# A hybrid attention and delta-rule layer: the triangular inverse held in blocks of 32, with products on four row groups, and all queues in a new order

## The reference

```python
A = jnp.einsum('bhnid,bhnjd->bhnij', kb, k) * decay_strict   # 64x64, strictly lower
sys = A + jnp.eye(C)
u = triangular_solve(sys, v * beta)                          # unit diagonal
w = triangular_solve(sys, kb * exp(G))
def step(state, xs):
    v_new = u_c - w_c @ state
    o = q_c @ state + qk_c @ v_new
    state = state * gl + k_c.T @ v_new
```

## Time and profile before

| what | value |
|---|---|
| median of 3 runs | 191.32 us (190.97 to 197.76) |
| profiled execution, its own time | 190.73 us |
| its span, first to last instruction | 188.9 us |
| granted clock, mean | 0.996 |

### The profile page before, as it was taken

The page is one execution under the profiler, slowest core; times in us unless marked ns, Lnnn a source line. Parts: engine busy times, 40 slices in busy tenths (PEclk is TensorE's granted clock), DMA queues, the critical chain, the costliest instruction groups (busy, mean ns, idle before and its releaser), DMA issues.

```text
span 188.9 us, 4380 instructions
## 1 busy us (share of the span) xinstructions
PE 178.0 (94%) x1718; PEld 161.5 (85%) x1718; DVE 141.5 (75%) x345; ACT 101.5 (54%) x195; POOL 77.5 (41%) x42
## 2 busy tenths in 40 slices
PE   7999989889999998999999999999999999999980
PEld 6769879789999998998998999999998987888850
DVE  0359699893459988998999787889689777858074
ACT  2645444439368878956562270455384448636230
POOL 2036627335687922985055068224913200810000
PEclk9999999999999999999999999999999999999998
DMA  5999999999519980300901807006942983020023
GB/s 160 403 386 394 393 409 407 407 397 404 218 16 367 395 328 8 114 0 2 323 14 17 319 8 212 13 0 220 362 201 78 344 356 119 14 97 0 3 111 111
DMA packets 12246, 38.41 MB, mean 203 GB/s; under 512 B 1473, under 2 KB 1857, under 8 KB 11714
## 3 DMA queue, kind: packets, MB, share of 16 engines
q1 hardware_dynamic: 12082, 37.61, 53.6%
q10 hardware_dynamic: 144, 0.52, 0.8%
HBM read 37.08 MB, written 1.05 MB: 202 GB/s over the span
## 4 chain that ended last, share of the span: by engine, by line
PE 69%; DVE 16%; DMA 6%; SPq 5%; issue 2%; ACT 1%; POOL 1%; DVEq 0%; POOLq 0%; ACTq 0%
PE bank L1395 16%; PE bank L1397 15%; PE bank L1396 15%; DVE cv L958 6%; DMA ada<-in_ada 6%; DVE bank L934 4%; SPq L351 3%; PE bank L1641 3%; PE bank L1630 3%; PE bank L1738 2%; PE bank L1745 2%; SPq L368 1%; PE bank L1754 1%; PE bank L1604 1%; PE bank L1666 1%
## 5 line engine op out<-in xcount | busy, mean ns | idle before, releaser
L474 POOL TENSOR_TENSOR wlo<-raw,whi 128x1024 fp32r<-128x1024 f32 (+1 forms) x25 | 58.1, 2334 | 62.2 <-ACT whi L543 62.2
L1395 PE MATMUL bank<-hhi,whi 128*128 128x256 f32 x218 | 63.1, 289 | 1.6 <-DVE hlo L906 1.1
L1396 PE MATMUL bank<-hhi,wlo 128*128 128x256 f32 x218 | 61.6, 283 | 0.0
L1397 PE MATMUL bank<-hlo,whi 128*128 128x256 f32 x218 | 61.6, 283 | 0.0
L1395 PEld LDWEIGHTS bank<-hhi,whi 128*128 128x128 f32 x218 | 41.7, 191 | 3.3 <-issue 1.8
L543 ACT ACTIVATE whi<-raw 128x1024 fp32r<-128x1024 f32 (+1 forms) x33 | 33.3, 1023 | 16.5 <-PE bank L1397 7.4
L1396 PEld LDWEIGHTS bank<-hhi,wlo 128*128 128x128 f32 x218 | 41.8, 192 | 0.0
L1397 PEld LDWEIGHTS bank<-hlo,whi 128*128 128x128 f32 x218 | 41.7, 191 | 0.0
L958 DVE SCALAR_TENSOR_TENSOR cv<-bank,convh,cv 128x255 f32<-128x255 f32 (+2 forms) x36 | 17.0, 481 | 5.6 <-ACT cv L609 4.6
L934 DVE SCALAR_TENSOR_TENSOR bank<-ada,sml,bank 128x256 f32<-128x256 f32 (+1 forms) x24 | 14.9, 621 | 0.7
L1157 DVE SCALAR_TENSOR_TENSOR accg<-ada,sml,accg 128x512 f32<-128x512 f32 x16 | 12.0, 751 | 2.7 <-DMA ada<-in_gate_w 2.3
(11 more groups left out here) (223 smaller groups left out, 337.6 us busy)
## 6 DMA issues: line engine op xcount, KB each, us to landing
raw<-in_w_rest SPq DMA_DIRECT2D x20, 512.0 KB, 4.8
ada<-in_ada SPq DMA_DIRECT2D x16, 256.0 KB, 7.1
ada<-in_ada SPq DMA_DIRECT2D x8, 512.0 KB, 12.0
ada<-in_gate_w SPq DMA_DIRECT2D x4, 1024.0 KB, 6.9
raw<-in_w_out SPq DMA_DIRECT2D x8, 512.0 KB, 5.7
raw<-in_w_qkv SPq DMA_DIRECT2D x5, 384.0 KB, 8.2
qkvs<-in_w_qkv SPq DMA_DIRECT2D x4, 384.0 KB, 11.2
cv<-in_w_qkv SPq DMA_DIRECT2D x4, 384.0 KB, 12.7
```

What stands on the lines that cost most here:

```text
L474: pool.tensor_tensor(split_u(wlo, n), raw_u(n), split_u(whi, n).bitcast(F32), ALU.subtract).then_inc(lo_done, 1)
L1395: pe.matmul(out, a[0][ia], b[0][ib], start=start, stop=False, skip_group_check=skip)
L1396: pe.matmul(out, a[1][ia], b[0][ib], start=False, stop=False, skip_group_check=skip)
L1397: return pe.matmul(out, a[0][ia], b[1][ib], start=False, stop=stop, skip_group_check=skip)
```

## The change

The inverse is held as `t32`, 128 partitions by 4 heads by 32 columns: the partitions of a quarter (32 tokens) hold that quarter's own diagonal block alone. Levels 1 to 4 stay inside those blocks. A step is now 16 matmuls of 32x32 with 16 columns, four quarters after each other on four row groups and four column groups, so 32 records. DVE's operations there have half the columns (`turn` 128, `mask_z` and `merge` 64). Level 0 takes one DVE operation more. Level 5 is written apart: `last_z_products` and `last_x_products` are 8 matmuls of 32x32 with 32 columns each, ACT copies z out of PSUM (`z_copy`), DVE spreads `t32` into `tt` (`spread`) and writes the lower left block (`last_merge`). `DVE_LO` shrinks from 12 units to 5, so POOL does units 5, 9, 11, 14, 21, 36, 40 and 41 now and DVE does unit 32. All five lists of calls are ordered anew.

```diff
-        DVE_LO = (5, 9, 11, 14, 21, 31, 35, 36, 40, 41, 42, 43)
+        DVE_LO = (31, 32, 35, 42, 43)
...
+            def z_copy(t):
+                act.wait_ge(z_ready, NT * (LEVELS - 2) + t + 1)
+                for c in range(2):
+                    q = quarter(2 * c)
+                    act.activation(heads(zt, t)[q], blocks(2 + 2 * t, 0, HALF)[q], ACT.Copy).then_inc(last_z, 1)
...
             def merge(l, t):
                 dve.wait_ge(x_ready, NT * (l - 1) + t + 1)
-                x_t = blocks(2 + 2 * t, 256, HALF).rearrange("p h (n b) -> p (h n) b", b=1 << l)
-                dve.tensor_tensor(heads_odd(tt, t, l), heads_odd(tt, t, l), x_t, ALU.subtract).then_inc(t_done, 1)
+                x_t = blocks(2 + 2 * t, 256, QUART).rearrange("p h (n b) -> p (h n) b", b=1 << l)
+                dve.tensor_tensor(heads_odd(t32, t, l), heads_odd(t32, t, l), x_t, ALU.subtract).then_inc(t_done, 1)
+
+            def spread(t):
+                dve.wait_ge(t_done, NT * (LEVELS - 2) + t + 1)
+                dve.tensor_tensor(heads(tt, t).rearrange("p h (a j) -> p h a j", a=2), heads(t32, t).unsqueeze(2).to_broadcast([P, DH, 2, HALF]),
+                                  cst[:, C_OWN:C_OWN + 2].unsqueeze(1).unsqueeze(3).to_broadcast([P, DH, 2, HALF]), ALU.mult)
+
+            def last_merge(t):
+                dve.wait_ge(x_ready, NT * (LEVELS - 2) + t + 1)
+                for c in range(2):
+                    q = quarter(2 * c)
+                    ins = dve.tensor_scalar(heads(tt, t)[q, :, HALF:], blocks(2 + 2 * t, 256, HALF)[q], -1.0, None, ALU.mult)
+                ins.then_inc(t_done, 1)
...
@@ z_products @@
-                    for c in range(2):
-                        r = rows_of(c)
-                        ins = pe.matmul(blocks(b, 0, HALF)[r, h, :], am[r, i, :], odd(tt[r, i, :], l), start=True, stop=True)
+                    for n in range(4):
+                        q, o = quarter(n), n % 2 * HALF
+                        ins = pe.matmul(blocks(b, 0, QUART)[q, h, :], am[q, i, o:o + HALF], odd(t32[q, i, :], l), start=True, stop=True)
@@ x_products @@
+                    for n in range(4):
+                        q = quarter(n)
+                        ins = pe.matmul(blocks(2 + 2 * t, 256, QUART)[q, h, :], ti32[q, i, :], zt[q, i, 0:QUART], start=True, stop=True)
...
+            def last_z_products(t):
+                pe.wait_ge(t_done, NT * (LEVELS - 2) + t + 1)
+                for h in range(DH):
+                    i = t * DH + h
+                    for c in range(2):
+                        ins = pe.matmul(blocks(2 + 2 * t, 0, HALF)[quarter(2 * c), h, :], am[quarter(2 * c + 1), i, 0:HALF], t32[quarter(2 * c + 1), i, :],
+                                        start=True, stop=True)
+                ins.then_inc(z_ready, 1)
```

More of the change, by code:

```diff
@@ L495, in _ @@
             lo(4)
+            lo(5)
             lo(6)
@@ L527, in _ @@
             lo(39)
+            lo(40)
+            lo(41)
         @block.scalar
@@ L1321, in _ @@
             mask_z(2, 1)
-            q_decayed(1)
             merge(2, 0)
@@ L1333, in _ @@
             mask_z(4, 0)
-            v_tokens(1)
             turn(4, 1)
@@ L1337, in _ @@
             merge(4, 0)
+            merge(4, 1)
+            spread(0)
+            spread(1)
             turn(5, 0)
-            merge(4, 1)
-            mask_z(5, 0)
             turn(5, 1)
-            mask_z(5, 1)
-            merge(5, 0)
-            merge(5, 1)
+            v_tokens(1)
+            gated_heads(1)
+            last_merge(0)
+            last_merge(1)
             rope(2)
-            gated_heads(1)
+            lo(31)
+            rope(3)
             gate_sums(0, 0, 4)
-            rope(3)
-            lo(31)
+            gate_sums(0, 4, 8)
+            state_update(0)
             maxima(2)
-            gate_sums(0, 4, 8)
+            q_decayed(1)
+            lo(32)
             normalise(2)
-            state_update(0)
+            gate_sums(1, 0, 4)
+            gate_sums(1, 4, 8)
+            gate(1)
             heads_lo(0)
-            gate_sums(1, 0, 4)
-            heads_lo(1)
-            gate_sums(1, 4, 8)
+            gated_heads(2)
             lo(35)
-            gate(1)
-            gated_heads(2)
             maxima(3)
             gate_lo(0)
+            normalise(3)
             state_update(1)
-            normalise(3)
-            heads_lo(2)
             gate(2)
             gate(3)
-            lo(36)
-            gated_heads(3)
-            state_update(2)
-            o_sums(0)
-            o_scale(0)
-            gate_lo(1)
-            gate_rows(0)
+            o_sums(0)
+            state_update(2)
+            gate_rows(0)
+            o_scale(0)
+            heads_lo(1)
+            heads_lo(2)
+            gate_lo(1)
+            gated_heads(3)
             heads_lo(3)
-            o_gate(0)
             gate_rows(1)
@@ L1855, in _ @@
             half(3)
+            k_turn(0)
             cum()
-            k_turn(0)
             k_turn(1)
@@ L1864, in _ @@
             half(7)
+            rows(0)
             scores(0)
-            rows(0)
             half(8)
@@ L1870, in _ @@
             half(9)
-            v_turn(0)
             p_turn(0)
@@ L1874, in _ @@
             pv(0)
+            v_turn(0)
             z_products(1, 0)
@@ L1884, in _ @@
             x_products(2, 1)
-            v_turn(1)
             z_products(3, 0)
             z_products(3, 1)
+            v_turn(1)
             p_turn(1)
```

252 lines of the change are left out of this document (133 added, 119 removed).

## The result

| | before | after |
|---|---|---|
| median, runs beside each other | 191.2 us | 199.05 us (198.68 to 199.17, 4 runs) |
| ratio | | **1.041** [1.039, 1.0434] |
| span, mean clock of the profiled run | 188.9 us, 0.996 | 197.0 us, 0.941 |

A forecast was written before the change was run, and what follows sets the result against it. PE, busy 94% at full clock, was taken to bound the kernel. From 190.73 us, gains of 2.9, 1.9 and 0.4 gave 185.5, stated as 185.7 for the median; range 182.8 to 190.0.

The forecast's parts named there:

- Term 1: In the inverse, smaller steps on four row groups at once gain 2.9 us, bounds 0 and 4.3.
- The forecast loop: One inverse step with the array's latency, DVE's operation and two hand-offs takes 0.86 us, binding instead of PE.
- two row groups: Rival in the inverse: only two row groups run at once, a step takes 0.62 us, run 189.1; chance 0.06.
- one at a time: Rival in the inverse: records into one bank queue at 39 ns, 1.25 us a step, run 200.3; chance 0.03.
- bound by issue: Rival in the inverse: a record costs 33 ns whatever its size, 1.05 us a step, run 196.8; chance 0.04.
- Term 2: Early PE waits for DVE: earlier `ada` pieces and low parts given to POOL gain 1.9 us, bounds 0 and 2.7.
- the first half of the term: Before the inverse: earlier `ada` pieces make piece 3's sum 1.0 us earlier, clearing PE's 0.83 us wait.
- Term 3: At the sums, `k_turn(0)` ahead of `cum` fills PE's 0.82 us wait for `zz`: gain 0.4 us, bounds 0 and 0.8.
- The costs put at nothing: POOL's extra low parts, DVE's added work, DVE's work behind 117 us and the end were counted as free.
- Given back later: Rival behind the inverse: DVE's `gate_sums` or loads come late, half the gain lost, 188.3 us; chance 0.13.
- ACT held by unit 28: Rival in the inverse: `hi(28)` ahead of `probs(1)` makes level 3 5.4 us or more late, about 190.9; chance 0.06.
- Level 5's gain of 0.55: Last level of the inverse: 2.6 us where it took 3.16, a gain of 0.55 us within the inverse's total.

The follow-up runs named there:

- e6: Kernel before, with unneeded bursts of small matmuls between dense ones behind its last matmul; longer by design, read in the profile alone, no time given.
- e12: Changed kernel without heads 1 and 3 in the z and x products of levels 1 to 4, plus 21 unneeded dense matmuls between steps: 190.65 us.
- e14: Changed kernel with low parts of units 5, 9, 11 and 14 made by DVE again: ratio 1.042.
- e10: Kernel before with only `ada` piece 3 and the first half of piece 4 issued one weight unit earlier: ratio 1.003.
- e11: Kernel before with `k_turn(0)` ahead of `cum` and the last level's z and x products on 32 rows: ratio 1.015.
- e13: Kernel before with only the last level's z and x products on 32 rows: ratio 1.0003.
- e1: Changed kernel with the inverse of before, keeping the new order and new split of low parts: 193.4 us, ratio 1.012.
- e2: New inverse in the order and split of low parts of the kernel before: 201.2 us, ratio 1.053.
- e3: Changed kernel with three unneeded dense matmuls ahead of each of seven inverse steps, 21 in all: 200.0 us, ratio 1.047.
- e4: Changed kernel with `half(11)` cut into four parts of six dense matmuls spread over levels 2 to 4: 199.4 us, one execution.
- e7: Changed kernel with part of its warm-up issued as 22 small matmuls, 60 more PE instructions at the start: 200.7 us.
- e8: Changed kernel with heads 1 and 3 left out of the z and x products of levels 1 to 4: 192.5 us.
- e9: Kernel before with five unneeded DVE operations ahead of the first merge of levels 1, 3 and 4: 207.5 us.

## Why the prediction was wrong

**Term 1** (-2.9 us) failed, though its mechanism is there. Four row groups do run at once: in e6 229 records take 2.09 us, less 0.2 for the last one's own duration 8.3 ns each, and a step of 32 in the changed kernel starts within 0.27 us, from 105.54 to 105.81, forecast 0.31:

```profile
105.54 0.44 PE L1658 MATMUL bank<-t,am 32*32 32x16 f32 x32
105.81 0.96 PE L1669 MATMUL bank<-zt,ti 32*32 32x16 f32 x64
106.62 0.94 PE L1658 MATMUL bank<-t,am 32*32 32x16 f32 x64
```

The forecast loop held too, as long as instructions were there: at 2.4 GHz the x steps of level 1 and the z steps of level 2 took 0.81 and 0.84 us (105.81, 106.62, 107.46), forecast 0.86, where a pair took 1.05.

DVE's operation on 64 columns takes 0.22 us, forecast 0.19. The Trainium skill's "TensorEngine Tiling (Array Packing)", section Restrictions and Gotchas, has the rule that different row tiles cannot access one PSUM bank at once. The Trainium skill's "TensorE: Matmul & The Clock Gate", section "Wait — 56ns, not 53.3ns?", has the floor of about 25 ns from start to start. As prices for this step both are contradicted by these rows: four row groups, each with partitions of its own in one bank, start 8.3 ns apart. The rivals "two row groups", "one at a time" and "bound by issue" did not come about: the last asked for the price of one record, 33 ns, and that is 8. The step of the sum that failed is "A new step ... is 0.31 us" taken sixteen times: it held for one step and not for a level, because PE's instruction stream was left out as a resource. Twice the instructions in half the time was visible in the order of the instructions, 32 records a step for 16; so were the instruction packets in the profile's DMA part. It costs 5.0 us. With 2.2 to 2.7 us from packet to resumption and some 127 records a piece, a price of under about 20 ns a record outruns the supply; that is an estimate from these runs, and the forecast's own 0.31 us a step, 10 ns a record, lay under it. Of the rivals, "one at a time" (200.3) and "bound by issue" (196.8) came nearest to the 199.05 measured, by luck: neither mechanism came about.

The second part left out is the clock. The earlier trace rows showed it granted in full, and the sum took that as a property of the chip, when it was one of the work. In the stretch at 1.2 GHz the chain of waits has these pieces (start, us, what):

```profile
111.41 1.04 PE bank L1614 x4
112.46 1.28 PE bank L1794 x6
...
121.29 1.06 PE bank L1803 x4
122.35 0.43 PE bank L1804 x4
122.78 0.99 PE bank L1690 x32
```

The kernel before has 0.59 and 0.81 us for the first two (`v_turn` and `p_turn` of one tile) and 0.81 for the next two together. With `half(11)`, 4.06 us where 24 x 0.12 = 2.88 were counted, the dense pieces alone lost 0.45 + 0.47 + 0.68 + 1.18 = 2.8 us. The small steps at this level, 0.95 to 1.0 a pair where 0.62 to 0.86 were counted, lost about 1 more; by this estimate the clock cost some 3.8. By subtraction, 7.0 - 5.0 - 3.8 = -1.8 us is what the smaller steps saved: an estimate, but of the sign of Term 1 and, for the gain, about two thirds of its size. e12 bounds it from the other side: from `pv(0)` to `w_products` it takes 19.6 us with 2.5 of filler, 2.9 of `half(11)` and one stop of 0.6 us, so 13.6 without them, where the kernel before takes 17.75; but that is with half of the products.

**Term 2** (-1.9 us) became +1.2 at `cum`. `acc` did come sooner, as said: PE's waits for it fell from 1.7 to 0.9 us, and the one of 1.06 for `hlo` is gone. In their place came three for POOL's low parts, 2.3 us, though a low part takes POOL 2.36 us where it took 2.33, and the clock stood at its 1.2 GHz level for 3.4 us from 37.4. "Such a unit is ready about 1.2 us later ... the ring of four slots lets it be made two units ahead" is the sentence that failed: the waits show that the units were not ahead of PE, whatever made them late (by e14 not the split alone). And by e10 the first half of the term was wrong by itself, since a piece of `ada` moved forward moves weights back that PE wants as soon.

**Term 3** (-0.4 us): PE waits 0.3 us for `qkvs` ahead of `k_turn(0)` where it waited 0.8 for `zz`, about as forecast. e11 shows what the same move can cost where DVE has a low part to make: 2.1 us.

**The costs put at nothing** behind the inverse held: from `gate_sum(0)` to the end it takes 32.4 us, before 32.5. (The 78.65 us of DVE given there for the time behind 117 us are those of 72 to 165 us.) "Given back later" did not happen, and neither did "ACT held by unit 28": `probs(1)` begins at 104.19 where it began at 103.47, less late than the inverse itself. Level 5's gain of 0.55 is 0.14 in e13, where ACT's copies are not in the way.

## What to carry to other kernels

Count the instructions of a PE stretch as well as its nanoseconds: where more than a hundred small fp32 records came at 8 to 14 ns each, the stream of instructions was the bound, and at 30 ns it was not. The sign is a stop in the middle of a step that the profile puts down to "issue" and that moves with the count of instructions ahead of it. A stop or a thin stretch on PE costs twice, once by itself and once by the clock over the dense work behind it; look at the granted clock of that work before a gain is summed up. And an operation of VectorE beside one of GpSimd has no duration of its own: read which of the two starts first before you move either.

## What the runs showed of the hardware

- PE's instructions come in 16 KB packets, 126 to 128 matmul records of fp32 apart; in 18 stops of 9 profiles PE resumes 2.2 to 2.7 us behind the start of the last packet (changed kernel, e1 to e4, e6, e7, e12, e14). Records of 8.3 and 14 ns in bursts of 256 ran into such stops, records of 30 ns did not (e6). One stop of e1 put down to "issue", 1.0 us up to 144.96, comes 4.2 us behind it and is not explained.
- 32x32 tiles on four row groups start 8.3 ns apart on average over 229 records, all into one bank.
- The granted clock fell to its 1.2 GHz level in thin stretches without a stop (e8) and behind a pause of 1.4 us with the old steps (e9), and held with 21 dense matmuls among the same thin steps (e12). In e6 it fell as well, at 189.7 for 3.4 us behind a stop that ended at 188.4, though dense work had started again by then.
- On DVE a low part of 1024 columns took 1.22 or 3.40 us, by whether it began ahead of POOL's or behind it (kernel before, e11); five operations of 128 columns took 1.59 or 5.72 (e9).
